# Sixteen dots of the third token tile moved ahead of the first one-hot build, in a hybrid encoder step

## The reference

```python
q = (hb @ w_pq).reshape(t, PEER_HEADS, 2, D_HALF)            # 8 heads, 2 halves
s = jnp.einsum('thpd,pnd->thpn', q, sub_keys)                # 128 key scores per half
sv, si = lax.top_k(s, PEER_TOPK)                             # top 16 of each half
cand = sv[:, :, 0, :, None] + sv[:, :, 1, None, :]
cidx = si[:, :, 0, :, None] * N_KEYS + si[:, :, 1, None, :]
tv, tpos = lax.top_k(cand.reshape(t, PEER_HEADS, 256), PEER_TOPK)
eidx = jnp.take_along_axis(cidx.reshape(t, PEER_HEADS, 256), tpos, axis=-1)   # 8 x 16 experts a token
g = jax.nn.softmax(tv, axis=-1)
u, vv = jnp.take(u_tab, eidx, axis=0), jnp.take(v_tab, eidx, axis=0)
act = jax.nn.gelu(jnp.einsum('td,ted->te', hb, u))
out = jnp.einsum('te,ted->td', g * act, vv)
```

## Time and profile before

| | |
|---|---|
| median of 3 runs | 4218.97 us (4212.77 to 4226.31) |
| the profiled execution | 4225.73 us, span 4223.9 us |
| granted TensorE clock, mean | 0.922 |
| TensorE / VectorE / ScalarE / GpSimd busy | 86% / 66% / 11% / 26% |
| moved by DMA | 1402.68 MB, mean 332 GB/s |
| dots (L1850) | 640, 2.29 us each |
| table product (L1112) | 4096 matmul records, 2048 for each pair |

### The profile page before, as it was taken

How to read it: one execution, slowest core, us unless ns; L and a number is a source line. 1 busy time by engine, 2 the same in 40 slices (tenths; PEclk the granted TensorE clock), 3 DMA queues, 4 the chain that set the end, 5 groups by cost and what they waited for, 6 DMA issues and landing times.

```text
span 4223.9 us, 34888 instructions
## 1 busy us (share of the span) xinstructions
PE 3631.7 (86%) x12495; PEld 2046.3 (48%) x12495; DVE 2777.5 (66%) x5036; ACT 450.4 (11%) x1083; POOL 1112.4 (26%) x862
## 2 busy tenths in 40 slices
PE   4699989987986899697789999999768999996991
PEld 0466667776542664354633444444354344443440
DVE  2138862238778977861977766776898676655677
ACT  1100012210000320101800000000161000000000
POOL 1100000006454334450043222222313322231233
PEclk6899999998997779798999999999869999998995
DMA  9977834459999999993199999999948999999996
GB/s 352 218 254 243 265 121 143 130 183 392 404 401 405 371 325 375 368 368 120 42 411 421 419 421 407 419 421 421 377 158 334 413 421 421 420 417 395 421 414 271
DMA packets 377072, 1402.68 MB, mean 332 GB/s; under 512 B 22416, under 2 KB 187480, under 8 KB 239397
## 3 DMA queue, kind: packets, MB, share of 16 engines
q0 software_dynamic: 116784, 831.77, 49.7%
q1 hardware_dynamic: 259552, 564.69, 36.1%
q10 hardware_dynamic: 576, 4.19, 0.2%
HBM read 1370.26 MB, written 31.81 MB: 332 GB/s over the span
## 4 chain that ended last, share of the span: by engine, by line
DMA 47%; PE 25%; DVE 14%; issue 11%; POOL 2%; ACT 1%; another core or an unknown queue 0%; SPq 0%; DVEq 0%; POOLq 0%; ACTq 0%
DMA R<-in_u_experts,MS 32%; PE bank L757 9%; DMA R<-in_v_experts,MS 9%; DVE R L1760 3%; PE bank L939 3%; PE bank L946 3%; PE bank L885 3%; DMA R<-in_w_ada 2%; DVE R L1850 2%; DVE R L1962 2%; POOL R L653 2%; PE bank L796 1%; DMA R<-in_w_out 1%; PE bank L711 1%; DMA R<-in_w_pq 1%
## 5 line engine op out<-in xcount | busy, mean ns | idle before, releaser
L653 POOL DMA_INDIRECT R<-in_u_experts,MS x640 | 899.9, 1406 | 1867.3 <-DVE MS L1850 1534.6
L1850 DVE CUSTOM_DVE_ANT_0 R<-R 128x2048 f32<-128x2048 f32 x384 | 880.6, 2293 | 418.0 <-DMA R<-in_u_experts,MS 402.4
L1112 PE MATMUL bank<-R,RB 128*128 128x512 f32 x2304 | 1015.6, 598 | 77.3 <-DMA R<-in_v_experts 77.3
L1112 PE MATMUL bank<-RB 128*128 128x512 f32 x1792 | 778.2, 592 | 0.0
L1112 PEld LDWEIGHTS bank<-R,RB 128*128 128x128 f32 x2304 | 438.9, 192 | 643.9 <-issue 547.5
L1850 DVE CUSTOM_DVE_ANT_0 R<-R,RB 128x2048 f32<-128x2048 f32 x256 | 585.4, 2287 | 118.8 <-DMA R<-in_u_experts,MS 118.0
L757 PE MATMUL bank<-RB,R 128*128 128x256 f32 (+1 forms) x2048 | 513.4, 412 | 51.1 <-DMA R<-in_w_pq 25.7
L1112 PEld LDWEIGHTS bank<-RB 128*128 128x128 f32 x1792 | 340.5, 190 | 428.5 <-issue 428.5
L757 PEld LDWEIGHTS bank<-RB,R 128*128 128x128 f32 x2048 | 392.8, 193 | 165.1 <-issue 33.7
L1962 DVE SCALAR_TENSOR_TENSOR R<-R,MS 128x2048 f32<-128x2048 f32 x128 | 301.1, 2352 | 190.1 <-DMA R<-in_v_experts,MS 188.6
L939 PE MATMUL bank<-RB,R 128*128 128x384 f32 x1024 | 338.5, 491 | 15.3 <-DMA R<-in_w_in 9.7
(11 more groups left out here) (294 smaller groups left out, 2334.3 us busy)
## 6 DMA issues: line engine op xcount, KB each, us to landing
R<-in_v_experts SPq DMA_DIRECT2D x144, 1024.0 KB, 9.1
RB<-in_v_experts SPq DMA_DIRECT2D x112, 1024.0 KB
R<-in_w_ada SPq DMA_DIRECT2D x48, 2048.0 KB, 12.7
R<-in_w_in SPq DMA_DIRECT2D x32, 2048.0 KB, 17.9
R<-in_w_out SPq DMA_DIRECT2D x16, 2048.0 KB, 11.5
R<-in_w_pq SPq DMA_DIRECT2D x16, 2048.0 KB
R<-in_u_experts,MS POOLq DMA_INDIRECT x640
RB<-in_x_prompt POOLq DMA_DIRECT2D x6, 1024.0 KB, 15.3
```

The lines of the kernel that those rows point to most:

```text
L653: pool.indirect_dma_start(dst, None, table, bass.IndirectOffsetOnAxis(ap=expert[T_ % 2][:, c:c + 1], axis=0)).then_inc(signal, 16)
L1112: x = pe.matmul(PB[4 * h + q][:, :], W[:, i, h * P:(h + 1) * P], vring[slot][:, q * PW:(q + 1) * PW], start=(i == 0), stop=(i == NKEY - 1))
L1850: V.tensor_tensor_reduce(u, u, x1[t] if t < TX else h2c, 1.0, 0.0, ALU.mult, ALU.add, dots[t % 2][:, h * TOPK + s:h * TOPK + s + 1]).then_ ...
```

## The change

- `DRAIN` goes; AHEAD = 16 and HEADS = 3 come. VectorE makes dots 256 to 271 before the first build, with x1[2] (where h2 of tile 2 still lies) as the other factor. Their experts are chosen from the scores in place: the first three heads of tile 2 are read from `SY`, groups 16 and 17 during the 16 dots of group 15. SP saves and reloads only the other five heads of that tile.
- The first build stands at n = 272 and has no selection steps in it. The second stands whole at n = 512, behind `drain`; both sets of picks are turned before it.
- On ScalarE `gate_exp(0)` and `gelu(0)` move ahead of the Y tiles' `row_squares`; `gelu(3)` and `load_h2(4)` ahead of `copy_turned(2)`.
- In the residual loop VectorE makes 4 dots behind each of the first 9 parts, 2 behind the tenth, and then `norm_tile(2)` and one dot, `norm_tile(3)` and one dot, behind the last two parts: 212 dots before `norm_tile(4)`.
- `vstY` has six buffers, so ScalarE does not wait for a store there.
- `iota_row` moves to another place, and GpSimd fills it when the attention is over.

```diff
-    DRAIN = 492
+    AHEAD = 16
+    HEADS = 3
...
-        vstY = VS[:, 0:1024].rearrange("p (b n) -> p b n", b=2)
+        vstY = [VS[:, 0:512], VS[:, 512:1024], *(rb(UB + 1024 + i * PW, PW) for i in range(4))]
...
             sp.wait_ge(s_se, 32)
-            for t in range(TX, T):
+            rest = slice(HEADS * 2 * NKEY, D)
+            sp.dma_start(S_d[TX][:, rest], SY[:, 0, 2 * HEADS:]).then_inc(s_Ss, 16)
+            for t in range(TX + 1, T):
                 sp.dma_start(S_d[t], SY[:, t - TX]).then_inc(s_Ss, 16)
             sp.wait_ge(s_Ss, 16 * TY)
-            sp.dma_start(Sc, S_d[TX]).then_inc(s_Sin, 16)
+            sp.dma_start(Sc[:, rest], S_d[TX][:, rest]).then_inc(s_Sin, 16)
...
                 if g == TX * NPH:
-                    pool.wait_ge(s_se, 4 * NPH)
+                    pool.wait_ge(pv_done, 2 * NH)
...
-                turn_picks(2 * pair)
-                if pair == 0:
-                    turn_picks(1)
-                scatter_tokens(2 * pair)
-                if pair:
-                    turn_picks(3)
-                scatter_tokens(2 * pair + 1)
+                for t in (2 * pair, 2 * pair + 1):
+                    turn_picks(t)
+                for t in (2 * pair, 2 * pair + 1):
+                    scatter_tokens(t)
                 dense(pair)
...
-                if v >= 2:
-                    act.wait_ge(s_vsty[v % 2], 16 * (v // 2))
-                A(vstY[:, v % 2], PB[v][:, :], ACT.Copy).then_inc(z_free, 1)
+                A(vstY[v], PB[v][:, :], ACT.Copy).then_inc(z_free, 1)
...
+            gate_exp(0)
+            gelu(0)
             for t in range(TX, T):
                 row_squares(t, x1[t], 4 + 16 + 9 + t - TX + 1)
...
-            gate_exp(0)
             gate_exp(1)
-            gelu(0)
             gelu(1)
             copy_turned(0)
             copy_turned(1)
...
             gate_exp(3)
+            gelu(3)
+            load_h2(4)
             copy_turned(2)
+            copy_turned(3)
             act.wait_ge(s_acc, 32)
             keep_W(2)
-            gelu(3)
-            load_h2(4)
-            copy_turned(3)
             keep_W(3)
...
-                    if t < 2:
-                        dve.wait_ge(s_se, 2 * h + 2)
-                    elif h == 0:
+                    if here:
+                        dve.wait_ge(s_se, 2 * h + 2 if t < TX else 16 + 2 * h + 2)
+                    elif h == (HEADS if t == TX else 0):
                         dve.wait_ge(s_Sin, 16 * (t - 1))
...
-            def first_burst():
-
-                for n in range(64):
+            def burst(pair):
+
+                for n in range(64 * pair, 64 * pair + 64):
                     one_hots(n)
-                    if n < 36:
-                        choose(2 * NPH + n // 18, n % 18)
...
                 if n == TX * P:
+                    dve.wait_ge(s_h2, TX + 1)
+                if n == TX * P + AHEAD:
                     for k in range(4):
                         weigh_picks(1, k)
                     dve.wait_ge(s_row, 1)
                     V.memset(ones, 1.0)
                     ch.link(CP(iota_row, iota_row.bitcast(U32)))
-                    first_burst()
-                if n == DRAIN:
-                    drain()
+                    burst(0)
+                    dve.wait_ge(s_h2in, 16)
                 if n == TP * P:
                     for k in range(4):
                         weigh_picks(3, k)
-                    for q in range(P // 4):
-                        one_hots(3 * (P // 4) + q)
+                    drain()
+                    burst(1)
...
+                x = x1[t] if n < TX * P + AHEAD else h2c
...
+                if g == 15:
+                    for q in range(s * 36 // TOPK, (s + 1) * 36 // TOPK):
+                        choose(16 + q // 18, q % 18)
...
-                if DRAIN + 2 <= n < TP * P:
-                    per = TP * P - DRAIN - 2
-                    m = n - DRAIN - 2
-                    for q in range(m * 32 // per, (m + 1) * 32 // per):
-                        one_hots(2 * (P // 4) + q)
...
-                steps(4)
-            dve.wait_ge(s_A2, 3)
-            for t in range(TX, T):
-                dve.wait_ge(s_sh2, 16 if t < TP else 16 * (1 + NB))
-                norm_tile(t, A2Y[0 if t < TP else 1], B2Y[0 if t < TP else 1])
+                if v < 3 * TY:
+                    steps(4)
+                elif v == 3 * TY:
+                    steps(2)
+                    dve.wait_ge(s_A2, 3)
+                    dve.wait_ge(s_sh2, 16)
+                elif v < 4 * TY:
+                    norm_tile(TX + v - 3 * TY - 1, A2Y[0], B2Y[0])
+                    steps(1)
+            dve.wait_ge(s_sh2, 16 * (1 + NB))
+            norm_tile(TP, A2Y[1], B2Y[1])
             steps(NG * TOPK - at_dot[0])
```

More of the change, by code:

```diff
@@ L182, in hybrid_encoder_step @@
         dots = [tk(P) for _ in range(2)]
-        first, second, weight = ([rb(31744 + (3 * t + i) * P, P) if t < TX else late(P) for t in range(T)] for i in range(3))
+        picks = [[rb(31744 + (3 * t + i) * P, P) for i in range(3)] for t in range(TX)]
+        picks.append([late(P) for i in range(3)])
+        iota_row = late(P)
+        picks += [[late(P) for i in range(3)] for t in range(TX + 1, T)]
+        first, second, weight = ([p[i] for p in picks] for i in range(3))
         turned = [late(3 * P).rearrange("p (o t) -> p o t", o=3) for i in range(2)]
-        iota_row = late(P)
         tv2, ti2, tf2 = tk(32), tk(32).bitcast(U32), tk(32)
@@ L427, in values_out @@
                     dst = kvo["v", 0][TX + t] if TX + t < TP else kvo["v", 1]
-                    sp.dma_start(dst[:, j * PW:(j + 1) * PW], vstY[:, v % 2]).then_inc(s_vsty[v % 2], 16)
+                    sp.dma_start(dst[:, j * PW:(j + 1) * PW], vstY[v]).then_inc(s_vsty[v % 2], 16)
             for n in range(12):
@@ L1332, in _ @@
                     head_out(h - 2)
-            for t in range(TX, T):
-                row_squares(t, x1[t], 4 + 16 + 9 + t - TX + 1)
-            for t in range(TX, T):
-                keep_h2T(t, h2TY, t - TX)
-            keep_queries(1, SY, TY)
             def gate_exp(t):
@@ L1346, in gelu @@
                 A(dots[t % 2], dots[t % 2], ACT.Gelu_apprx_tanh).then_inc(gel_rdy, 1)
+            gate_exp(0)
+            gelu(0)
+            for t in range(TX, T):
+                row_squares(t, x1[t], 4 + 16 + 9 + t - TX + 1)
+            for t in range(TX, T):
+                keep_h2T(t, h2TY, t - TX)
+            keep_queries(1, SY, TY)
             def copy_turned(t):
@@ L1664, in choose @@
                 at = slice(h * TOPK, (h + 1) * TOPK)
-                keys = SX[:, t, 2 * h:2 * h + 2].rearrange("p r n -> p (r n)") if t < 2 else Sc[:, h * 256:(h + 1) * 256]
+                here = t < TX or (t == TX and h < HEADS)
+                kept_S = SX[:, t] if t < TX else SY[:, 0]
+                keys = kept_S[:, 2 * h:2 * h + 2].rearrange("p r n -> p (r n)") if here else Sc[:, h * 256:(h + 1) * 256]
                 rows2 = [keys[:, p * P:(p + 1) * P] for p in range(2)]
@@ L1843, in step @@
                         weigh_picks(3, k)
-                    for q in range(P // 4):
-                        one_hots(3 * (P // 4) + q)
-                if h == 0 and s == 0 and t >= TX:
+                    drain()
+                    burst(1)
+                if h == 0 and s == 0 and t > TX:
                     dve.wait_ge(s_h2in, 16 * (t - 1))
                 u = ux[n % NU]
+                x = x1[t] if n < TX * P + AHEAD else h2c
                 dve.wait_ge(u_in[n % NU], 16 * (n // NU + 1))
-                V.tensor_tensor_reduce(u, u, x1[t] if t < TX else h2c, 1.0, 0.0, ALU.mult, ALU.add,
+                V.tensor_tensor_reduce(u, u, x, 1.0, 0.0, ALU.mult, ALU.add,
                                        dots[t % 2][:, h * TOPK + s:h * TOPK + s + 1]).then_inc(dots_done, 1)
```

## The result

| | before | after |
|---|---|---|
| median, both on one chip | 4219.57 us (4212.77 to 4226.31) | 4147.61 us (4143.43 to 4156.72) |
| the profiled execution | 4225.73 us, span 4223.9 | 4143.43 us, span 4141.7 |
| first product starts at | 2115.8 | 2081.5 |
| from there to the second product | 1074.8 | 1037.0 |
| from there to the end of the span | 1033.3 | 1023.2 |

The ratio is 0.9832, 95% interval 0.981 to 0.9855: 72 us faster, where 65 were forecast (4154 us, range 4122 to 4190). Between the two profiled executions there are 82 us: 34.3 ahead of the first product, 37.8 between the products and 10.1 behind the second one, where the program is the same.

A forecast was written before the change was run, and what follows sets the result against it. No engine bounds throughout: TensorE and DMA fill the products, VectorE sets the builds, and a gate wait stalls it before the first. Terms -11, -13 and -41 sum to -65 us: 4161 profiled, 4154 as median, range 4122 to 4190.

The forecast's parts named there:

- Later attention: Start of the later attention: six value buffers end TensorE's 29.9 us wait for ScalarE; -3 us, between 0 and -4.
- Norms earlier: Norms ahead of the key queries: the last ends at 1788 against 1790.4; -2.5 us, bounds -8 and +8.
- Gathers beside the key queries: Key queries: the last four w_pq loads meet the gathers, 2 us each; +8 us (0 to +20), scores end at 1983.
- The new wait: Before the first build: ScalarE waits 15 us (7.8 to 19) for the score saves; first distances at 1998, -11 us.
- First build: Build without selection steps: 32 pairs at 2.83 us take 90.6; -13 us, first product at 2091.8.
- Second build: Between the products, whole build behind the drain: new terms sum to 118.5 us against 159.8 us now; -41 us.
- The check by bytes: Check on the second build: 16 dots less behind the first build, 16.8 MB at 417 GB/s, 40.2 us.
- Key queries slip: Rival: four w_pq loads 6 us late each and saves at 19 put ScalarE's start at 2018; 4174 us, chance 0.15.
- Nothing in the way: Rival: key queries do not slip and saves take 8 us, start at 1983; 4139 us, chance 0.11.
- Cold TensorE: Rival: in the second build TensorE stays at its low clock for 20 pairs, losing 30 us; 4184, chance 0.06.
- Slower: Rival: x1 save and SP's queue in 1741:1983 are starved; 4240 us or so, chance 0.03.
- The 0.64 case: The forecast itself for the whole kernel: -65 us, 4154 us, chance 0.64.

The follow-up runs named there:

- E4: The changed kernel with two value buffers in place of six and ScalarE's waits for the stores: 4150.43 us, ratio 0.9826.
- E10: The changed kernel, unaltered, measured again on another chip: 4145.83 us, ratio 0.9815 to the kernel before.
- E3: The changed kernel with the norms in their old order, four dots behind every residual part and the three norms after the loop: 4147.93 us, ratio 0.9816.
- E5: The changed kernel with its second build spread out as before, drain at dot 492, the 16 dots ahead kept: 4177.02 us, ratio 0.9887.
- E7: The changed kernel with 32 dots ahead of the first build and four heads chosen in place: 4162.97 us, ratio 0.9844.
- E8: The changed kernel with ScalarE's waits for the saves moved from ahead of its first distances to its first copy into W: 4142.07 us, ratio 0.9793.
- E11: The changed kernel with SP's last x1 saves of tiles 2 and 3 issued one w_pq load earlier: 4142.57 us, ratio 0.9812.
- E6: The changed kernel with no dots ahead of the first build and two heads chosen in place: 4183.32 us, ratio 0.99.

## Why the prediction was right, and where it was off

The direction, the mechanism and the size were right: 4154 against 4147.6, with -24 ahead of the first product (measured -34.3), -41 between the products (-37.8), and nothing behind (-10.1, which the tails of the other runs put down to spread). The measured values below are those of the one profiled execution of `after`, where no other is named.

1. **Later attention, -3: wrong.** See E4. The step read 29.9 us of TensorE's wait and 2.35 us of VectorE's and still took off 3; the first head began 2 us later. The bound of 0 was the right value: VectorE's own dots set the time.
2. **Norms earlier, -2.5: measured -4.** The x1 save kept VectorE until 1759.06 (I had 1757), the last norm ended at 1786.6 (1788), and TensorE's run of key queries starts at 1791.04, where before, the profile has 1795.0. E10 has 1783.8, so this value alone is uncertain by some 8 us. E3 puts the whole of this order at 0 to 6 us.
3. **Gathers beside the key queries, +8: the step that failed.** I took 2 us for each of four more w_pq loads, from the 3.58 and 1.33 us of the earlier trace rows. In `after` there is one wait for w_pq in all, 1.73 us, although the gathers run throughout. In the other executions with this code (E5, E7, E8, E10) the waits are 1.9 to 6.1 us in all, where before has 4.9: no growth, and not 8. The landing took 20.3 us at the median, under the some 23 us of TensorE's work on the other half, which covers it. The scores ended at 1969.8 (1966 to 1970 in the other four) and not at 1983. A part of the 7 us by which TensorE's key queries are shorter than before is the clock: their first 96 matmuls took 33.62 us in before, with a granted clock of 0.93 in 1795:1828, and 31.23 us in `after`, with 1.00 in 1791:1822. What I overlooked is that with a load issued in time, a slower load costs nothing until it is longer than the work that covers it; two waits by 1892 were no rate. The row behind my term was there, and I extended it past the place in which it held.
4. **The new wait, 15 us: it took 20.4.** SP issued at 1969.87 and saw the saves landed at 1990.24. That is over my upper bound of 19: the saves are 2.75 MB, with the load of h2c ahead of them in the same queue and four gathers beside them. The gathers are what makes them slow: E3, with the last gather issued 15 us before, has 9.5 us for the same transfers, and E10, with gathers, 19.3; a 1 MB save took 17.2 us at the median in `after`, 7.6 in E3 and 7.8 in before. The Trainium skill, page "DMA: Bandwidth & Descriptors", section "Anatomy of one DMA", fitted its formula to transfers issued by GpSimd, while SP issues these; its estimate of 10.7 us for 3.8 MB alone is near E3's 9.5 and says nothing of the case with gathers. Late saves took back 5 of the 13 us that the early scores gave: ScalarE's first distances are at 1990.30, 7.7 us ahead of my 1998. That two errors of opposite sign met there is luck.
5. **What set that start.** The 16 dots ended at 1981.2. I had 1976 and a few us more; the working seems to take the 3 us of the later attention off twice (1788 less 3 is the 1785 from which it starts), and once gives 1979. VectorE's weights freed TensorE at 1983.14. In ScalarE's row the wait for the saves is the last one, 5.73 us, right behind one of 10.62 us for VectorE's dots. That looks like two bounds within 6 us of each other, but E10 shows that the saves decide: there the same code had the dots' part done 10 us earlier, waited 14.12 us for the saves and started only 1.6 us earlier. In E11 it is the same. In E7, with 16 dots more, it is the dots (53.41 us of ScalarE's wait).
6. **First build, 93.6 us from the first distances to the product: measured 91.2.** The last pairs take 2.83 us as before; stretches at 2.74 (from 2039.20 to 2041.94, say) and 2.04 us to the first piece in place of 3 make the difference. First product at 2081.5, forecast 2091.8: the error of point 3, less that of point 4, and this.
7. **Second build.** From the first product to the drain I had 927.0 us and the profile has 930.9 (3012.35 less 2081.47), because 9 dots end behind the product (2988.0), where before has 3, which with the four more would be 7. From the drain to the second product I had 106.5 and it took 106.2. ScalarE waited 7.53 us for the acc saves, of my 8. Sum -37.8 for -41. The check by bytes, 40.2, meets E6's 40.4. By the Trainium skill's HBM limit, page "DMA: Bandwidth & Descriptors", section "Specifications", the 16 dots would be an estimated 46.9 us: that row halves a stack's bandwidth between two cores, and here one core ran. E6 measured 40.4, and the products' windows 415 GB/s.
8. **The rivals.** Key queries slip: no, 1.73 us. Nothing in the way: for the key queries, yes; for the saves, no. Cold TensorE: only for the first groups. Behind 29.27 us of idling the granted clock was 0.50 in 3017:3029, the lower of the two levels (1.2 and 2.4 GHz), and 8 matmuls took 2.08 us; over the second build it was 0.89, near the upper one, with 2.19 us for a pair's 16 matmuls at its end. Slower: nothing was starved.

The 0.64 case came out, some 7 us below its number, with wrong terms of both signs in it.

## What to carry to other kernels

Price a stall by the work that could be done in it, not by its length: here 102 us of waiting were worth 12 alone, and 51 when 16 dots and their selection could be pulled into it. A move whose gain passes through a later meeting point (here the drain at dot 492) needs that point moved too, or the engines idle there for what was won, and pulling more ahead stops paying where the idle time does: 0, 16 and 32 dots gave 4183, 4148 and 4163, the last two not apart beyond the noise. A transfer that has grown slower costs only what exceeds the work that covers it.

## What was not expected of the hardware

- SP's loads of w_pq, 2 MB each, kept up with TensorE beside a full stream of gathers: 1.73 us of waits in 178 us of key queries (6.1 in 185 in E10), DMA at 398 GB/s in 1880:1983.
- The saves to DRAM were slow only beside the gathers: 2.75 MB, behind 1 MB of h2c in the same queue, took 19 to 21 us with gathers in flight (`after`, E5, E8, E10) and 9.5 without (E3). By the byte they are no slower than the loads: h2c and the saves are 3.8 MB and took 22.4 us from h2c's issue at 1967.83, and a load of 2 MB took 20.3. The loads have work to cover them, and the saves have none.
- A short wait cost TensorE more than its length here. In E10 it idled 5.54 us for w_pq, and the 16 matmuls behind took 7.54 us, with a granted clock of 0.74 in 1853.5:1862; behind 1.73 us of idling, in `after`, they took 5.43. In E11 it was 3.34 us of idling and 8.48.
- The first product takes 906 to 908 us in before, `after` and E7, though in E7 VectorE waits for the last 21 us of it. The value pieces keep their pace, and the gathers have what is left.
